# Reordering a hybrid attention and HGRN2 step on one core: a decay scan, exponentials, key pages, sample state and the output mix

## The reference, cut to what matters

```python
q, k, v, a_gate, iq, iw, ik, hq, hg, hk, hv, h_gate = branch_inputs(x, ...)   # rms_norm(x) @ w_in, split
# A: sparse attention. index scores -> each query keeps its 256 best keys -> softmax over them
score = sum_h relu(iq_h . ik) * iw_h ; idx = top_k(score, 256)
a_out = softmax(q . k[idx] + bias[q_pos - idx]) . v[idx]
# B: gated linear recurrence, by chunks; f = lb + (1 - lb) * sigmoid(h_f), hg = log f, hk = 1 - f
b = cumsum(hg) ; S' = exp(b_last) * S + (hk * exp(b_last - b))^T v ; o = (q exp(b)) S + intra(q, k, decay) v
# sample rows: the same with a paged cache of 1024 past keys, and with the state S given per row
y = x + concat(a_out * silu(a_gate), rms_norm(o) * silu(h_gate)) @ w_out
```

## Time and profile before

| | |
|---|---|
| median of 3 runs | 941.49 us |
| profiled execution | 938.64 us, span 936.8 us |
| TensorE (PE) busy | 884.6 us, 94% |
| VectorE (DVE) busy | 633.9 us, 68% |
| ScalarE (ACT) busy | 411.2 us, 44% |
| GpSimd (POOL) busy | 324.5 us, 35% |
| granted TensorE clock, mean | 0.984 |
| TensorE waits, the five longest after 300 us | 6.08, 4.32, 4.12, 3.07, 2.01 us |

### The profile page before, as it was taken

The page is one execution under the profiler, slowest core; times in us unless marked ns, Lnnn a source line. Parts: engine busy times, 40 slices in busy tenths (PEclk is TensorE's granted clock), DMA queues, the critical chain, the costliest instruction groups (busy, mean ns, idle before and its releaser), DMA issues.

```text
span 936.8 us, 17973 instructions
## 1 busy us (share of the span) xinstructions
PE 884.6 (94%) x6482; PEld 792.6 (85%) x6482; DVE 633.9 (68%) x1193; ACT 411.2 (44%) x1203; POOL 324.5 (35%) x309
## 2 busy tenths in 40 slices
PE   4999999999999899999997998899999997999998
PEld 4989887899999899989987897566796667998998
DVE  4436878899889988999899867855453236535111
ACT  6546670345646764665535454333342225322100
POOL 1434443238442934383737231700011004311210
PEclk9999999999999999999997999899999999999999
DMA  7220202111022112211231527543135334232322
GB/s 260 64 65 21 65 24 93 46 27 38 30 68 86 36 63 68 85 44 54 80 102 35 143 80 216 137 120 105 32 94 176 116 103 147 70 115 79 126 86 74
DMA packets 79421, 81.32 MB, mean 87 GB/s; under 512 B 20234, under 2 KB 68026, under 8 KB 79082
## 3 DMA queue, kind: packets, MB, share of 16 engines
q1 hardware_dynamic: 77722, 74.97, 26.5%
q0 software_dynamic: 1616, 5.25, 2.2%
HBM read 62.85 MB, written 17.34 MB: 86 GB/s over the span
## 4 chain that ended last, share of the span: by engine, by line
PE 46%; DVE 20%; issue 20%; DMA 7%; POOL 3%; ACT 2%; DVEq 1%; SPq 0%; POOLq 0%; ACTq 0%
PE psum L1105 11%; DMA index_keys_T<-in_cache_ikt,index_page_rows 6%; PE psum L1075 5%; PE psum L1946 5%; PE psum L1943 4%; DVE flag L1736 4%; PE psum L1125 3%; PE psum L1061 3%; PE psum L1167 3%; DVE flag L826 3%; PE psum L1827 2%; DVE bit_kept L1750 2%; PE psum L1040 2%; POOL w_low L450 2%; DVE bits_so_far L1753 2%
## 5 line engine op out<-in xcount | busy, mean ns | idle before, releaser
L1946 PE MATMUL psum<-w_high,xT_high 128*128 128x256 f32 x720 | 206.5, 287 | 12.2 <-ACT stage L1536 9.5
L1946 PE MATMUL psum<-w_low,xT_high 128*128 128x256 f32 x720 | 203.2, 282 | 0.0
L1946 PE MATMUL psum<-w_high,xT_low 128*128 128x256 f32 x720 | 203.0, 282 | 0.0
L1736 DVE TENSOR_SCALAR_CACHE_REDUCE flag<-scores,candidate 128x384 f16<-128x384 f32 (+2 forms) x192 | 181.7, 946 | 6.9
L1946 PEld LDWEIGHTS psum<-w_high,xT_high 128*128 128x128 f32 x720 | 129.0, 179 | 16.0 <-issue 6.4
L1946 PEld LDWEIGHTS psum<-w_high,xT_low 128*128 128x128 f32 x720 | 129.0, 179 | 2.4
L1946 PEld LDWEIGHTS psum<-w_low,xT_high 128*128 128x128 f32 x720 | 129.0, 179 | 2.3
L450 POOL TENSOR_TENSOR w_low<-w_raw,w_high 128x1024 fp32r<-128x1024 f32 (+2 forms) x46 | 100.2, 2199 | 79.6 <-ACT w_high L1429 79.4
L771 ACT ACTIVATE prob<-psum,neg_max 128x1024 f32<-128x1024 f32 (+7 forms) x64 | 47.4, 740 | 148.5 <-DVE neg_max L978 148.5
L1943 PE MATMUL psum<-xT_high,w_high 128*128 128x384 f32 (+3 forms) x312 | 102.8, 329 | 1.2 <-DVE xT_low L1670 1.2
L1943 PE MATMUL psum<-xT_high,w_low 128*128 128x384 f32 (+3 forms) x312 | 100.4, 322 | 0.0
(11 more groups left out here) (289 smaller groups left out, 1919.3 us busy)
## 6 DMA issues: line engine op xcount, KB each, us to landing
w_raw<-in_w_main SPq DMA_DIRECT2D x40, 512.0 KB, 4.3
page_keys<-in_cache_kt SPq DMA_DIRECT2D x64, 128.0 KB, 2.6
page_values<-in_cache_v SPq DMA_DIRECT2D x64, 128.0 KB, 2.3
x_rows<-in_x_prompt SPq DMA_DIRECT2D x8, 512.0 KB, 5.4
x_res<-in_x_prompt SPq DMA_DIRECT2D x32, 128.0 KB
out<-y_rows SPq DMA_DIRECT2D x32, 128.0 KB
hgate_spill<-stage SPq DMA_DIRECT2D x16, 128.0 KB
ho_spill<-ho_rows SPq DMA_DIRECT2D x4, 512.0 KB, 3.7
```

What stands on the lines that cost most here:

```text
L1736: dve.tensor_scalar(JK[:, 0:w], sc, threshold(k), None, op, ALU.add, accum_out=CNT[:, k:k + 1]).then_inc(s["dve_chain"], 1)
L1946: last = pe.matmul(ps(BANK[n], w, rows(i)), x[:, k, row0(i):row0(i) + rows(i)], ww[:, sl, k, 0:w], start=first, stop=final)
```

## The change

- **ScalarE, exponentials in one unit.** `EXP_AT` is gone. For every j, part 0 comes behind the evacuation of job 6, parts 1 and 2 behind that of job 7, and `prep_heads` behind that of job 8, all in the unit behind the HGRN2 unit.
- **VectorE, scan(3).** New order behind the roots: sample rounds 2 to 4, `dve_norm(0)`, scan(3), `dve_norm(1)`, sample rounds 5 to 19. The sample rows' norm comes one build later, and the low part of the bias one build earlier (its high part on ScalarE one job earlier).
- **Keys.** The first two of the 16 key products stand ahead of the first scores, the others in steps 0 to 13, one in each. Their first two page loads are issued in unit 15, at q = 10 and 12. The sample rows' q and k have another place in memory, so the page buffers rotate plainly.
- **GpSimd, sample state.** Three operations over 8 sample rows at once (128 x 2048) become 24 over one row each (128 x 256).
- **Mix.** VectorE's `mix_low` comes one step after ScalarE's `mix_high`; the weight rounding at steps 34 and 44 moves to 35 and 45, and the last output product from step 62 to 63.
- **Start.** GpSimd waits for the first three x scales before it makes the first low weights.
- **Small ones.** ScalarE's relu of the sample index scores comes one job earlier; its query copy of the last tile comes ahead of the load of the exponential's table; three waits on SyncE move from the key pages to the first mix load.

```diff
-KEYS_AT = [-1] + [1 + int(0.8 * n) for n in range(1, 2 * SB)]
+KEYS_AT = [-1, -1] + list(range(2 * SB - 2))
-OUT_AT = [41, 43, 45, 47, 49, 50, 52, 54, 55, 58, 62]
-HIGH_AT = {34: 0, 44: 1}
+OUT_AT = [41, 43, 45, 47, 49, 50, 52, 54, 55, 58, 63]
+HIGH_AT = {35: 0, 45: 1}
-BIAS_AT = JOB0[LAST] + 13
+BIAS_AT = JOB0[LAST] + 12
-EXP_AT = (6, 6, 6, 5)
...
             SIDE.setdefault(m, []).append(("mix", x))
+            SIDE.setdefault(m + 1, []).append(("mix_low", x))
...
         def key_buffer(n):
-            return (0, 2, 3, 1)[n % 4]
+            return n % 4
...
-            if n == 0:
+            if n < 2:
                 sp.wait_ge(s["weights_low_ready"], 2 * NU)
-            elif n < 3:
+            elif n < 4:
                 sp.wait_ge(s["job_done"], JOB0[NU])
...
-            if q == 4:
-                load_sample_rows(sp)
-            if q == 6:
-                load_key_pages(sp, 0)
+            if q == 9:
+                load_sample_rows(sp)
+            if q in (10, 12):
+                load_key_pages(sp, (q - 10) // 2)
...
-                link(gp.tensor_tensor(S0T[:, :, :, :], S0T[:, :, :, :], spread(FS), ALU.mult))
-                link(gp.tensor_tensor(VBT[:, :, :, :], VBT[:, :, :, :], spread(KSS), ALU.mult))
-                gp.tensor_tensor(S0T[:, :, :, :], S0T[:, :, :, :], VBT[:, :, :, :], ALU.add).then_inc(s["sample_state_ready"], 1)
+                for b in range(SB):
+                    gp.tensor_tensor(S0T[:, b, :, :], S0T[:, b, :, :], spread(FS, b), ALU.mult)
+                    last = gp.tensor_tensor(VBT[:, b, :, :], VBT[:, b, :, :], spread(KSS, b), ALU.mult)
+                link(last)
+                for b in range(SB):
+                    last = gp.tensor_tensor(S0T[:, b, :, :], S0T[:, b, :, :], VBT[:, b, :, :], ALU.add)
+                last.then_inc(s["sample_state_ready"], 1)
...
-            dve_norm(dve, link, chain, 0)
-            dve_norm(dve, link, chain, 1)
-
         def dve_builds(dve, link, chain):
...
-                if i == 2:
+                if i == 3:
                     dve_norm_sample(dve, link)
-                if i == NT - 2:
+                if i == NT - 3:
                     dve.wait_ge(s["bias_high_ready"], 1)
...
-                elif kind == "mix":
+                elif kind == "mix_low":
                     mix_low(b)
...
+            for side in SIDE[-1]:
+                sample(*side)
             scores(0)
...
+            gp.wait_ge(s["x_scale_ready"], 3)
             split_w(gp, 0)
...
-                if u - 2 in HGU:
-                    prep_exp(HGU.index(u - 2), 2)
...
-                    if u - 1 in HGU and q - EXP_AT[HGU.index(u - 1)] in (0, 1):
-                        prep_exp(HGU.index(u - 1), q - EXP_AT[HGU.index(u - 1)])
-                    if u - 1 == HGU[NG - 1] and q == NT:
-                        prep_heads(NG - 1)
-                    if u - 2 in HGU[:NG - 1] and q == 1:
-                        prep_heads(HGU.index(u - 2))
+                    if u - 1 in HGU and q == 6:
+                        prep_exp(HGU.index(u - 1), 0)
+                    if u - 1 in HGU and q == 7:
+                        prep_exp(HGU.index(u - 1), 1)
+                        prep_exp(HGU.index(u - 1), 2)
+                    if u - 1 in HGU and q == NT:
+                        prep_heads(HGU.index(u - 1))
...
                     if n in BUILD_AT:
+                        act_query_tile(act, BUILD_AT[n])
                         if n == JOB0[NU] - 1:
                             act.activation(RI[:, 0:1], IDN[:, 0:1], ACT.Exp)
-                        act_query_tile(act, BUILD_AT[n])
...
             dve_rows(dve, link, chain)
-            sample_rounds(2, 7)
+            sample_rounds(2, 5)
+            dve_norm(dve, link, chain, 0)
             scan(3)
-            sample_rounds(7, 20)
+            dve_norm(dve, link, chain, 1)
+            sample_rounds(5, 20)
```

More of the change, by code:

```diff
@@ L249, in hymba_step @@
         W0 = cur[0]
-        QRS, KRS, _ = over(W0 - 4096, ("q_rows_sample", [512], F32), ("k_rows_sample", [KVH, 2, HD], F32))
         KP = [over(W0 - 8192 + 4096 * x, (f"page_keys_{x}", [2, 512], F32))[0] for x in range(4)]
@@ L282, in hymba_step @@
         CU = sb("flag_count", [PAST + 8], F16)
+        QRS, KRS, _e = over(JK0, ("q_rows_sample", [512], F32), ("k_rows_sample", [KVH, 2, HD], F32))
+        assert _e <= cur[0]
         IKT2, _ = over(S0 + SCW * 4, ("index_keys_T2", [PAST], F32))
@@ L474, in load_sample_rows @@
         def load_sample_rows(sp):
-            sp.wait_ge(s["weights_low_ready"], 2 * NU)
+            sp.wait_ge(s["qk_normed"], 3)
             sp.dma_start(KRS[0:SB, :, 0, :], d_k[T:TT, :].rearrange("t (h d) -> t h d", d=HD)).then_inc(s["sample_rows_in"], 16)
@@ L483, in key_buffer @@
         def key_buffer(n):
-            return (0, 2, 3, 1)[n % 4]
+            return n % 4
         def load_key_pages(sp, n):
             b, first, x = n % SB, n // SB * 4, key_buffer(n)
-            if n == 0:
+            if n < 2:
                 sp.wait_ge(s["weights_low_ready"], 2 * NU)
-            elif n < 3:
+            elif n < 4:
                 sp.wait_ge(s["job_done"], JOB0[NU])
-            elif n == 3:
-                sp.wait_ge(s["sample_q_transposed"], 1)
-                sp.wait_ge(s["new_key_products_ready"], 1)
-                sp.wait_ge(s["early_outputs_stored"], 48)
             else:
@@ L512, in sp_last_unit @@
                 load_rows(sp, (q - 1) // 2)
-            if q == 6:
-                load_key_pages(sp, 0)
-            if q == 12:
+            if q == 9:
+                load_sample_rows(sp)
+            if q in (10, 12):
+                load_key_pages(sp, (q - 10) // 2)
+            if q == 14:
                 sp.wait_ge(s["sample_qk_normed"], 1)
@@ L579, in sp_tail @@
             store_keys(sp, NT - 1)
-            for n in range(1, 2 * SB):
+            for n in range(2, 2 * SB):
                 load_key_pages(sp, n)
@@ L592, in sp_tail @@
             sp.wait_ge(s["new_prob_diag_ready"], 1)
+            sp.wait_ge(s["sample_q_transposed"], 1)
+            sp.wait_ge(s["new_key_products_ready"], 1)
+            sp.wait_ge(s["early_outputs_stored"], 48)
             load_mix(0)
@@ L646, in sample_state, with spread @@
                 gp.wait_ge(s["states_in"], 48)
-                def spread(x):
-                    return bass.AP(x, 0, [[NG * SB, P], [1, SB], [SB, NG], [0, HD]])
-                link(gp.tensor_tensor(S0T[:, :, :, :], S0T[:, :, :, :], spread(FS), ALU.mult))
-                link(gp.tensor_tensor(VBT[:, :, :, :], VBT[:, :, :, :], spread(KSS), ALU.mult))
-                gp.tensor_tensor(S0T[:, :, :, :], S0T[:, :, :, :], VBT[:, :, :, :], ALU.add).then_inc(s["sample_state_ready"], 1)
+                def spread(x, b):
+                    return bass.AP(x, b, [[NG * SB, P], [SB, NG], [0, HD]])
+                for b in range(SB):
[5 more added lines that the diff above has]
+                last.then_inc(s["sample_state_ready"], 1)
                 gp.wait_ge(s["sample_state_ready"], 1)
@@ L1178, in pe_tail @@
                     scores(m + 1)
-                if m == 0:
-                    for side in SIDE[-1]:
-                        sample(*side)
                 if m >= 2:
@@ L1603, in _ @@
                         index_relu(m)
-                    if n == SAMPLE_SUM_AT:
+                    if n == SAMPLE_AT:
                         act.wait_ge(s["early_outputs_stored"], 32)
```

## The result

| | before | after |
|---|---|---|
| median of 5 executions | 941.63 us | 934.87 us |
| repeated in e9, beside more executions | 939.16 us | 935.74 us |
| profiled execution, span | 936.8 us | 933.9 us |
| TensorE busy | 884.6 us | 882.5 us |
| VectorE's first build starts | 525.81 us | 530.21 us |

The ratio is 0.9921 (95% interval 0.9896 to 0.9946); repeated, it is 0.9960 (0.9930 to 0.9989). The change makes the kernel 3.4 to 6.8 us faster, where 14.8 us were forecast. The smaller number is the more likely one: over all executions on record the kernel before takes 938.4 us on average (136 executions) and the kernel after 935.1 us (17), and the first five of before all lie above that average. The median of 934.87 us lies just inside the forecast range of 918 to 935.5 us, and the repeated one of 935.74 us just outside.

What follows compares the result with a forecast made beforehand. TensorE's waits and clock losses were taken as the bound, with VectorE level at the second build. Terms 0.6 + 0 - 5.7 - 2.9 - 6.3 - 0.5 = -14.8 us, from the 941.5 median to 926.7 us; range 918 to 935.5.

Steps and rivals of the forecast that it cites:

- The bound: Whole kernel: TensorE's waits and clock losses set the end; TensorE and VectorE reach the second build together.
- Scan(3): VectorE's new order behind the roots: scan some 7 us sooner, TensorE's 6.08 us wait gone; +0.6 us, from -3 to +4.6.
- VectorE's arrival: At VectorE's first build, which TensorE's second build needs: -1.0 us, between -3 and +3.
- Exponentials and head copies: ScalarE, moved into one unit: TensorE's new waits covered by its slack before the second build; 0, bounds 0 and +3 us.
- Rows and keys: Attention: sample state by rows removes a 4.12 us wait, -5.7 us; key products fill a 4.32 us wait, -2.9 us.
- the third product: Third key product, wanted at about 588 us: its page loads, issued from 581 on, just in time or up to 2 us late.
- rival 4: GpSimd's sample state: rows don't let VectorE in, the -5.7 is lost; about 935 to 938 us, chance 0.06.
- Mix: Low part one step later: TensorE's five waits of 8.5 us shrink, GpSimd's gain limits tile 2; -6.3 us, from -11.7 to -2.
- Start: GpSimd's wait before its first low weights: TensorE starts 1.1 us sooner; -0.5 us, from -1.1 to 0.
- the relu: ScalarE's relu one job earlier: frees TensorE where VectorE bounds; 0 us.
- Rival 3: Head copies, late pages and the norm beside GpSimd each come to their bad end; about 935 us, chance 0.10.
- marks named for "wrong": First build after 528 or before 521 us, page waits, waits at L1090, second long wait near 230, 320 or 414.

Runs made afterwards that it cites:

- e9: The kernel after, unchanged, profiled and timed again: 935.74 us beside 939.16 for the kernel before.
- e2: The kernel before with VectorE's new order around scan(3) alone: 939.61 us beside 936.31, ratio 1.0014.
- e14: The kernel before with GpSimd's weight splits and decay preparation in pieces of at most 256 elements a row: 939.58 us beside 938.91, ratio 1.0013.
- e17: The kernel before with VectorE's new order around scan(3) and GpSimd's work in pieces: 933.69 us beside 940.66, ratio 0.9950.
- e7: The kernel after with norm 1 ahead of scan(3) in place of behind it: 930.61 us beside 937.22, ratio 0.9933.
- e4: The kernel before with the low part of the mix one step later alone: 931.90 us beside 936.31, ratio 0.9941.
- e5: The kernel before with the three exponentials and the head copies in one unit alone: 941.19 us beside 937.22, ratio 1.002.
- e13: The kernel after with exponentials and head copies where they stood in the kernel before: 933.04 us beside 938.91, ratio 0.9943.
- e8: The kernel after with the third key product and all later ones one step later: 932.90 us beside 937.22, ratio 0.9959.
- e12: The kernel before with the key part alone and the two small moves on ScalarE: 933.18 us beside 939.16, ratio 0.9940.
- e3: The kernel before with the sample state by rows alone: 936.48 us beside 936.31, ratio 0.9971.
- e1: The kernel before with GpSimd's wait for the first three x scales alone: 936.24 us beside 936.31, ratio 0.998.
- e6: The kernel after without GpSimd's wait at the start: 935.23 us beside 937.22, ratio 0.9967.
- e10: The kernel after with norm 1 ahead of scan(3) and the third key product one step later: 928.60 us beside 939.16, ratio 0.9900.
- e16: The kernel after with GpSimd's weight splits and preparation in pieces: 925.07 us beside 938.91, ratio 0.9857.
- e15: The kernel after with norm 1 ahead of scan(3), third key product later, exponentials at their old place, GpSimd's work in pieces: 920.37 us beside 938.91, ratio 0.9808.

## Why the prediction was wrong, point by point

**The bound** was read rightly: TensorE's waits, and TensorE and VectorE together at the second build. e2, e14 and e17 show it.

**Scan(3).** This step failed in its size. The mechanism was right: the scan starts at 479.83 us (forecast near 478), the wait of 6.08 us is gone, a wait before the second build takes its place, with the clock at 0.50 behind it. The mis-sized term is VectorE's arrival: I took -1.0 us and it came 4.4 us later (525.81 to 530.21). Norm 1 takes 6.6 us beside GpSimd's preparation in place of 2.4; I had named this, and left it in the range. e7 returns 3.4 us of b-c. Alone the term is +3.1 us by the stretches of e2 (+1.4 and +1.7), forecast +0.6; the 1.7 us are a fall of the clock, and e4 had one there without the edit.

**Exponentials and head copies.** Forecast 0; this step failed in its mechanism. I looked for the cost in TensorE's waits and let its slack cover them. They are covered. But TensorE's place decides which of VectorE's steps GpSimd's splits meet and when the q rows land: 5.4 us of b-c in e5, 4.3 us in e13. With norm 1's 3.4 us, and less the wait of 1.80 us for the q rows that the new order saves, that is 5.9 to 7.0 us, somewhat more than the 5.5 us by which b-c grew (62.9 to 68.4).

**Rows and keys.** Forecast -5.7 and -2.9, measured -4.4 together. The step that failed is one term: the third product was called "just in time or up to 2 us late" and priced at nothing, and it cost 2.06 us of waiting and 1.8 us of low clock (3.68 us in place of 1.86). Its loads were issued from 587.51 us on and not from 581, and the product could start at 597.27 us. e8, without that wait, gives -9.5, so adding the two terms was no error: that keys alone also remove the wait of 4.12 us (e12) was not in the forecast, and is worth nothing where the rows have removed it. That the rows let VectorE in (rival 4) is shown by e3: 0.31 us, as against 3.42. For other trains of pieces it is not so (last section). The Trainium skill's rule (SBUF — State Buffer, section "Who interferes with whom"), that who comes first holds the shared ports for its instruction, agrees with both numbers.

**Mix.** Right in its mechanism. VectorE waits 2.03 us for GpSimd's gain at tile 2, as forecast, and TensorE 3.21 us behind it. -5.1 us between the two profiles, -4.2 on average, against -6.3. In the term's sum the 2.6 us are what goes of the first three waits (6.1 us), so 3.5 us were to stay; 3.21 and 0.63 us stayed. A wait of 1.49 us behind a copy at 854 us is new. VectorE's timeline:

```profile
781.57 1.75 DVE L875 TENSOR_TENSOR ho_in<-ho_in,ho_square_sums 128x512 f32<-128x512 f32 x1 [2.03 <-POOL hgate_in L671]
```

**Start.** TensorE starts 1.2 us sooner and the end doesn't move by more than the noise (e1, e6): what TensorE gains ahead of a place that VectorE sets is absorbed. I said so of the relu and not of the start.

**The rivals.** Rival 3 came, with all three of its parts (head copies, late pages, the norm beside GpSimd) at or beyond their bad ends, and its 935 us. I gave it 0.10 as if three mishaps had to meet; but the rows already spoke for each of them, so the likely values belonged into the sum. Of the marks named for "wrong", three were met: a first build later than 528 us, a key product that waits for its pages, and a wait near 414 us (2.64 us).

**The sum**, between the two profiled executions: c came 4.4 us later where 1.5 us sooner was forecast, the start among it (5.9 of the miss); c-d grew by 2.1 us, with 1.6 forecast (0.5); d-e shrank by 4.4 us, with 8.6 forecast (4.2); e-f by 5.1, with 6.3 forecast (1.2). That is 11.8 us, the whole way from -14.8 to -3.0. By the first medians the gain is larger (6.8 us), since the profiled execution of before was 3.0 us quicker than its median and that of after 0.8 us slower. a-b is 313 us in both profiles of the kernel after and 316.0 to 316.7 in e6, e7, e8 and e10, which have the same exponentials; how much of that is chance stays open. The prediction took 0.2% for what a measurement can tell here; the intervals are 0.5 to 1.1% wide.

## What to carry to other kernels

Where two engines reach a meeting point together, an edit that moves one of them can be worth nothing and two edits that move both can be worth 5 to 7 us (e2, e14, e17): measure them together. A small step with two SBUF inputs mostly cost what was left of GpSimd's instruction beside it (3.42 us beside one of 3.67, 0.31 us beside one of 0.61), so price a reordering by what each moved step will stand beside. Cutting GpSimd's long instructions helped, 10.7 us in e16, but count the long waits that stay. And put the likely value of a doubtful cost into the sum; don't leave it in the range because its row lies on the edge.

## What the runs showed of the hardware

**GpSimd's pieces do not always let VectorE in.** In e3, and for most small steps of e14 to e17, the wait is at most one piece (0.3 to 1.0 us). But each of the four kernels with pieces has two or three small steps that took 6 to 7.5 us: 6.92 and 6.86 us in e14; 6.97, 7.51 and 5.99 us in e15; 6.96, 6.75 and 7.38 us in e16; 6.90 and 6.84 us in e17. All ten began beside one of the four weight splits that GpSimd's multiplication `q_decayed` follows without a gap, and ended only behind that multiplication or the operations next to it. So what rival 4 feared for the sample state, where it did not happen, happens at these splits; eight of the ten lie in a-b. VectorE's timeline of e14, then GpSimd's:

```profile
231.25 6.92 DVE L1761 TENSOR_SCALAR bit_kept<-count,bit_value 128x6 int32<-128x6 f32 x1
```
```profile
228.43 5.57 POOL L450 TENSOR_TENSOR w_low<-w_raw,w_high 128x256 fp32r<-128x256 f32 x8
233.94 2.83 POOL L1323 TENSOR_TENSOR q_decayed<-q_decayed,hq 128x256 f32<-128x256 f32 x4
236.70 1.44 POOL L1331 TENSOR_TENSOR intra<-intra,intra_mask 128x256 f32<-128x256 f32 x2
```

The same of e16, in the stretch b-c:

```profile
501.94 7.38 DVE L833 TENSOR_TENSOR bits_so_far<-bits_so_far,bit_kept 8x1 int32<-8x1 int32 x1
```
```profile
501.00 5.54 POOL L450 TENSOR_TENSOR w_low<-w_raw,w_high 128x256 fp32r<-128x256 f32 x8
506.51 2.80 POOL L1322 TENSOR_TENSOR q_decayed<-q_decayed,hq 128x256 f32<-128x256 f32 x4
```

At others of these splits the small steps got in (0.59, 0.65 and 0.84 us in e14, near 323 us); why there and not here was not found. **Pieces cost GpSimd** 2.80 us for 4 x 256 elements, against 2.38 us for 1024 at once (weight splits). **The clock** fell to 0.50 at the second build of e4, behind waits of 0.89 and 0.70 us, and stayed at full speed there behind one of 0.71 us in the kernel before. It fell behind waits of 1.52 and 1.36 us in e9; in e12 waits of 1.52 and 1.44 us at the same place were followed by a product of 1.93 us at full clock:

```profile
592.79 1.93 PE L1124 MATMUL psum<-page_keys,q_padded 128*64 128x512 f32 x4 [1.44 <-DMA page_keys<-in_cache_kt]
```
